# Gated delta rule in a decoder layer: block turns of v and of the output, and the decay exponents, made another way

## The reference, cut to what matters

```python
qkv = silu(causal_depthwise_conv(concat([q, k, v]), conv_w))
g = cumsum(g.reshape(B, H, N, C), axis=-1)          # g = log of the decay, C = 64 tokens
decay = exp(where(causal, g[..., :, None] - g[..., None, :], -inf))
a_mat = where(strict, einsum('bhncd,bhnsd->bhncs', k_beta, k) * decay, 0.0)
sol = triangular_solve(a_mat + eye(C), concat([v * beta, k_beta * exp(g)]), unit_diagonal=True)
qk = einsum('bhncd,bhnsd->bhncs', q, k) * decay
# scan over chunks with a state S per head; then
o = rms_norm(o, norm_w) * silu(z)                   # goes into o @ w_branch_a
```

## Time and profile before

| | |
|---|---|
| three timed executions | 1939.5, 1939.63, 1939.84 us |
| span of the profiled execution, first to last instruction | 1937.5 us |
| busy: PE, PEld | 1922.7 us (99%), 1581.1 us |
| busy: DVE, ACT, POOL | 1365.1 us (70%), 935.0 us (48%), 101.1 us |
| granted TensorE clock, mean | 0.998 |
| DMA | 353.19 MB, mean 182 GB/s |

### The profile page before, as it was taken

How to read it: one execution, slowest core, us unless ns; L and a number is a source line. 1 busy time by engine, 2 the same in 40 slices (tenths; PEclk the granted TensorE clock), 3 DMA queues, 4 the chain that set the end, 5 groups by cost and what they waited for, 6 DMA issues and landing times.

```text
span 1937.5 us, 33061 instructions
## 1 busy us (share of the span) xinstructions
PE 1922.7 (99%) x11140; PEld 1581.1 (82%) x11140; DVE 1365.1 (70%) x1961; ACT 935.0 (48%) x1331; POOL 101.1 (5%) x296
## 2 busy tenths in 40 slices
PE   9999999999999999999999999999999999999997
PEld 7888887888888888888888888888888888888886
DVE  7779889797857777776566766577675466665556
ACT  6555565554455545455544445644443444443442
POOL 0102020010101111111000000000000000000000
PEclk9999999999999999999999999999999999999999
DMA  7444444444554545455655676555555555656555
GB/s 267 154 142 158 149 152 142 154 153 142 186 179 159 188 161 191 159 189 174 190 192 194 216 239 200 181 194 191 191 194 195 194 193 188 196 195 194 194 189 174
DMA packets 98013, 353.19 MB, mean 182 GB/s; under 512 B 10832, under 2 KB 11120, under 8 KB 97776
## 3 DMA queue, kind: packets, MB, share of 16 engines
q1 hardware_dynamic: 97904, 351.65, 55.4%
HBM read 349.51 MB, written 2.10 MB: 181 GB/s over the span
## 4 chain that ended last, share of the span: by engine, by line
PE 95%; DVE 2%; ACT 1%; issue 1%; DMA 1%; SPq 0%; DVEq 0%; ACTq 0%
PE pg L399 88%; PE B L399 5%; DVE gates L1212 1%; DMA raw<-in_weights 1%; PE B L493 0%; ACT whi L800 0%; DVE wlo L1204 0%; PE B L657 0%; ACT hraw L1086 0%; PE B L527 0%; ACT gates L1074 0%; PE B L666 0%; PE B L622 0%; ACT vda L1086 0%; ACT act_a L800 0%
## 5 line engine op out<-in xcount | busy, mean ns | idle before, releaser
L1204 DVE TENSOR_TENSOR wlo<-raw,whi 128x1024 fp32r<-128x1024 f32 (+1 forms) x640 | 779.4, 1221 | 452.1 <-ACT whi L800 433.8
L800 ACT ACTIVATE whi<-raw 128x1024 fp32r<-128x1024 f32 (+1 forms) x640 | 674.4, 1058 | 684.6 <-PE pg L399 673.0
L399 PE MATMUL pg<-whi,act_x 128*128 128x512 f32 x2960 | 950.5, 394 | 1.5 <-ACT whi L800 1.2
L399 PEld LDWEIGHTS pg<-whi,act_x 128*128 128x128 f32 x2960 | 555.3, 188 | 124.3 <-issue 8.9
L399 PE MATMUL pg<-wlo,act_x 128*128 128x512 f32 x1480 | 574.7, 390 | 0.0
L399 PE MATMUL pg<-whi,act_a 128*128 128x512 f32 x1632 | 504.8, 389 | 0.5 <-DVE act_a L1204 0.5
L399 PEld LDWEIGHTS pg<-whi,act_a 128*128 128x128 f32 x1632 | 306.3, 188 | 64.8 <-DVE act_a L1204 1.3
L399 PEld LDWEIGHTS pg<-wlo,act_x 128*128 128x128 f32 x1480 | 278.3, 188 | 53.3
L399 PE MATMUL pg<-wlo,act_a 128*128 128x512 f32 x816 | 317.5, 389 | 0.0
L399 PEld LDWEIGHTS pg<-wlo,act_a 128*128 128x128 f32 x816 | 153.2, 188 | 31.7
L399 PE MATMUL pg<-whi,act_b 128*128 128x512 f32 x512 | 158.4, 389 | 0.0
(11 more groups left out here) (230 smaller groups left out, 1106.5 us busy)
## 6 DMA issues: line engine op xcount, KB each, us to landing
raw<-in_weights SPq DMA_DIRECT2D x646, 512.0 KB, 3.8
gates<-in_ln_in SPq DMA_DIRECT2D x4, 512.0 KB, 5.9
gates<-in_ln_in SPq DMA_DIRECT2D x1, 2048.0 KB, 8.4
out<-gates SPq DMA_DIRECT2D x8, 256.0 KB, 2.8
raw<-in_weights SPq DMA_DIRECT2D x4, 256.0 KB, 4.6
cT<-in_xT SPq DMA_DIRECT2D x2, 512.0 KB, 7.2
qT<-in_xrow SPq DMA_DIRECT2D x2, 512.0 KB, 7.4
kT<-in_xrow SPq DMA_DIRECT2D x2, 512.0 KB, 6.3
```

What stands on the lines that cost most here:

```text
L399: return nc.tensor.matmul(o, l, r, start=start, stop=stop)
L800: return nc.scalar.activation(o, i, ACT.Copy, scale=scale)
L1204: return V.tensor_tensor(o, a, b, op)
```

## The change

v: one VectorE transpose of 32x32 blocks over all 128 partitions (slot 20) writes `stage`. SP stores `stage` to `turn_v` in DRAM, waits until it is stored, and loads it back with the blocks in their new places, as four transfers of 32 partitions each. The rows are scaled from there in slots 26 and 30 (before: behind the last turn in slot 31, and in slot 0 of the next body). The output of head groups 0 to 2: two such transposes (slot 11 of the next body), the same way through `turn_o` to `oT`, split in slots 24 and 25 (before: 29 and 30). Decays: one small product in body 0 gives every running sum of g; ScalarE stores its transpose to DRAM, and one broadcast transfer per body, started by ScalarE, fills `decm` with it. ScalarE then does a Relu of `g - sum` for each of 8 tiles of 128x128 and one exponential over all of them: in bodies 1 to 3 two Relus in each of slots 4 to 7 and the exponential in slot 7, in body 0 all of it in slot 13. The masks `g_hi`, `g_lo`, the 4 products and the old exponential are gone.

```diff
-OT_TURN = {11: 3, 12: 4, 14: 2, 18: 1, 20: 3, 21: 3}
-OT_HI = 29
-V_TURN = {21: 1, 22: 3, 23: 3, 27: 3, 28: 2, 29: 2, 30: 1, 31: 1}
+O_BLOCKS, V_BLOCKS = 11, 20
+O_HI = 24
+V_SCALED = (26, 30)
...
-ROWS = range(2, 6)
+DECAY = range(4, 8)
...
+        stage = tmp("stage", [P, 4, 8, SB])
+        oT = tmp("oT", [P, 4, 8, SB])
...
+        centre, sums = (flat(QKT[:, :, :])[:, i * P:(i + 1) * P] for i in range(2))
+        vtok = flat(kT[:, :, :]).rearrange("p (a q x) -> p a q x", a=4, x=SB)
+        turn_v, turn_o = (nc.dram_tensor(n, (4, SB, 4, 8 * SB), F32).ap() for n in ("turn_v", "turn_o"))
+        sums_out = nc.dram_tensor("sums_out", (NB, 8 * P), F32).ap()
...
-            with sp.Fori(2, out_m) as m:
+
+            def blocks_out(scratch, kept):
+                sp.dma_start(scratch.rearrange("a x b c -> (a x) (b c)"), stage[:, :, :, :].rearrange("p b q x -> p (b q x)")
+                             ).then_inc(kept, 16)
+
+            def blocks_in(scratch, dst, full):
+                for b in range(4):
+                    sp.dma_start(dst[b * SB:(b + 1) * SB], scratch[:, :, b].rearrange("a x (q i) -> x a q i", i=SB)
+                                 ).then_inc(full, 16)
+
+            def v_out(j):
+                sp.wait_ge(N["dve_vS"], 1 + j + 1)
+                blocks_out(turn_v, v_kept)
+
+            def v_in(j):
+                sp.wait_ge(v_kept, 16 * (j + 1))
+                blocks_in(turn_v, vtok, v_full)
+
+            def o_out(j):
+                sp.wait_ge(N["dve_oS"], 1 + j)
+                blocks_out(turn_o, o_kept)
+
+            def o_in(j):
+                sp.wait_ge(o_kept, 16 * j)
+                blocks_in(turn_o, oT, o_full)
+
+            for m in range(2, 7):
+                later(m)
+            v_out(0)
+            later(7, range(0, 2))
+            v_in(0)
+            later(7, range(2, 4))
+            with sp.Fori(1, NB) as j:
+                for i in range(3):
+                    later(8 * j + i)
+                later(8 * j + 3, range(0, 3))
+                o_out(j)
+                later(8 * j + 3, range(3, 4))
+                later(8 * j + 4, range(0, 1))
+                o_in(j)
+                later(8 * j + 4, range(1, 4))
+                later(8 * j + 5)
+                later(8 * j + 6)
+                v_out(j)
+                later(8 * j + 7, range(0, 2))
+                v_in(j)
+                later(8 * j + 7, range(2, 4))
+            with sp.Fori(NB * BODY // RING, out_m) as m:
...
+                    mm(B[3][:, 64:96], centre, g_all[:, :]).then_inc(N["pe_sc0"], 1)
+                if s == 9:
+                    pe.wait_ge(N["act_gc"], 1)
+                    nc.tensor.transpose(B[3][0:SB, P:2 * P], pz[:, 1, :], ident).then_inc(N["pe_gT"], 1)
...
-                if s == 12:
-                    pe.wait_ge(N["rows"], 1 + j + 1)
-                    if isinstance(j, int):
-                        pe.wait_ge(N["act_glo"], 1)
+                if s == 13:
+                    pe.wait_ge(N["act_silu"], 1 + 3 * j + 1)
...
-                    for t in range(TOK):
-                        mm(B[1 + t][:, :], after_r[:, :], flat(g_hi[:, 4 * t:4 * t + 4, :]), True, False)
-                        last = mm(B[1 + t][:, :], after_r[:, :], flat(g_lo[:, 4 * t:4 * t + 4, :]), False, True)
-                    last.then_inc(N["pe_dt"], 1)
-                if s == 13:
-                    pe.wait_ge(N["act_silu"], 1 + 3 * j + 1)
-                    pe.wait_ge(N["act_decay"], 1 + j + 1)
...
+                    for t in range(TOK):
+                        by_t = B[3][:, 64 + HEADS * t:64 + HEADS * (t + 1)].rearrange("p (j h) -> p j h", h=HB)
+                        a0 = SC["gc"][0] + 4 * t
+                        copy(scal[:, :, a0:a0 + 4], by_t)
+                        last = copy(pz[:, 1, :].rearrange("p (j t h) -> p j t h", j=NB, t=TOK)[:, :, t, :], by_t)
+                    last.then_inc(N["act_gc"], 1)
+                if s == 10:
+                    act.wait_ge(N["pe_gT"], 1)
+                    copy(sums[0:SB, :], B[3][0:SB, P:2 * P]).then_inc(N["act_gT"], 1)
+                    act.wait_ge(N["act_gT"], 1)
+                    act.dma_start(sums_out.rearrange("j (i c) -> (j i) c", c=P), sums[0:SB, :]).then_inc(sums_kept, 16)
+                if s == 11:
+                    act.wait_ge(sums_kept, 16)
+                    sums_in(0)
+
+            def sums_in(j):
+
+                act.wait_ge(N["dve_qk"], 1 + 2 * j)
+                act.dma_start(flat(decm[:, :, :]), sums_out[bass.ds(j, 1)].rearrange("o c -> (o c)").partition_broadcast(P)
+                              ).then_inc(sums_full, 16)
...
+            def decays(j, part, parts):
+
+                if part == 0:
+                    act.wait_ge(sums_full, 16 * (j + 1))
+                    act.wait_ge(N["dve_g"], 1 + j + 1)
+                for i in range(8 // parts * part, 8 // parts * (part + 1)):
+                    last = nc.scalar.activation(decm[:, i, :], decm[:, i, :], ACT.Relu, bias=gcur[:, i:i + 1], scale=-1.0)
+                if part == parts - 1:
+                    last.then_inc(N["act_past"], 1)
+                    act.wait_ge(N["act_past"], 1 + j + 1)
+                    nc.scalar.activation(decm[:, :, :], decm[:, :, :], ACT.Exp, scale=-1.0).then_inc(N["act_decay"], 1)
+
             def dn_build(j, s):
-                if s in ROWS and not isinstance(j, int):
-                    per = 16 // len(ROWS)
-                    if s == ROWS[0]:
-                        act.wait_ge(N["dve_g"], 1 + j + 1)
-                        act.wait_ge(N["pe_dt"], 1 + j)
-                    for i in range(per * (s - ROWS[0]), per * (s - ROWS[0] + 1)):
-                        last = nc.scalar.activation((g_hi if i < 8 else g_lo)[:, i % 8, :], c("same"), ACT.Copy,
-                                                    scale=gcur[:, i:i + 1])
-                    if s == ROWS[-1]:
-                        last.then_inc(N["rows"], 1)
-                if s == 12:
-                    act.wait_ge(N["pe_dt"], 1 + j + 1)
-                    act.wait_ge(N["dve_qk"], 1 + 2 * j)
-                    for t in range(TOK):
-                        last = nc.scalar.activation(decm[:, 4 * t:4 * t + 4, :], B4[1 + t], ACT.Exp)
-                    last.then_inc(N["act_decay"], 1)
...
+                    if isinstance(j, int):
+                        decays(j, 0, 1)
...
-                if not alone and s == OT_HI:
-                    act.wait_ge(N["dve_od"], 1 + j + 1)
-                    copy(hi(act_a, HB * j, HB), qT[:, :, :]).then_inc(N["act_oT"], 2)
+                if not alone and s == O_HI:
+                    act.wait_ge(o_full, 64 * (j + 1))
+                    copy(by_block(hi(act_a, HB * j, HB)), by_source(oT)).then_inc(N["act_oT"], 2)
...
+                if s == 10:
+                    dve.wait_ge(N["act_gc"], 1)
+                    g_next(0)
...
-                if s in V_TURN:
-                    at = sum(n for k, n in V_TURN.items() if k < s)
-                    if at == 0:
-                        dve.wait_ge(N["act_silu"], 1 + 3 * j + 2)
-                    for i in range(at, at + V_TURN[s]):
-                        a, b = divmod(i, 4)
-                        ins = V.transpose(heads_of(kT)[b * SB:(b + 1) * SB, :, :, a, :],
-                                          tokens_of(cT[:, 1])[a * SB:(a + 1) * SB, :, :, b, :])
-                    if i == 15:
-                        ins.then_inc(N["dve_vT"], 1)
+                if s == V_BLOCKS:
+                    dve.wait_ge(N["act_silu"], 1 + 3 * j + 2)
+                    if not isinstance(j, int):
+                        dve.wait_ge(o_kept, 16 * j)
+                    V.transpose(stage[:, :, :, :].rearrange("p b q x -> p q b x"),
+                                cT[:, 1].rearrange("p h (q b x) -> p (h q) b x", q=TOK, x=SB)).then_inc(N["dve_vS"], 1)
+                if s in V_SCALED:
+                    if s == V_SCALED[0]:
                         dve.wait_ge(N["pool_rinv"], 1 + j + 1)
-                        dve.wait_ge(N["dve_vT"], 1 + j + 1)
-                        v_scaled(j, 0)
+                        dve.wait_ge(v_full, 64 * (j + 1))
+                    v_scaled(j, V_SCALED.index(s))
...
+                if not alone and s == O_BLOCKS:
+                    dve.wait_ge(N["dve_oh"], 1 + 2 * j + 2)
+                    dve.wait_ge(v_kept, 16 * (j + 1))
+                    for t in range(TOK):
+                        last = V.transpose(stage[:, :, :, :].rearrange("p b (h t) x -> p h t b x", t=TOK)[:, :, t],
+                                           od[:, t].rearrange("p h (b x) -> p h b x", x=SB))
+                    last.then_inc(N["dve_oS"], 1)
...
+                if not alone and s == O_HI + 1:
                     dve.wait_ge(N["act_oT"], 1 + 2 * j + 2)
-                    tt(lo(act_a, HB * j, HB), qT[:, :, :], hi(act_a, HB * j, HB), ALU.subtract).then_inc(N["dve_oT"], 2)
```

(46 more changed lines are left out.)

37 lines of the change are left out of this document (16 added, 21 removed).

## The result

The changed kernel takes 1972.05 us (median of 5, 1970.47 to 1974.4) against 1939.84 (5, 1939.5 to 1939.99): ratio 1.0168, 95% interval 1.0157 to 1.018. Slower was forecast, but at 1954 us with 1966 as the upper end; the loss is 32.2 us where 14.4 were forecast. The way was right, the size wrong.

The account below looks back on a forecast made before the run. TensorE, busy 1922.7 of 1937.5 us, was taken as the bound. To 1939.6 us it added 11.4 for bodies 1 to 3 and 2.6 for body 0, TensorE's savings included: 1953.6, stated as 1954 us; range 1942 to 1966.

Parts of the forecast that it names:

- What bounds, what TensorE saves: TensorE bounds; dropping four products per body saves 3.7 us, body 0's additions cost 0.2 to 0.3: net -3.5 us.
- VectorE's saving is worth nothing: Fewer block transposes remove about 39 us of VectorE work, worth nothing on TensorE.
- SP's hold: Bodies 1 to 3: the output store waits on SP's queue ahead of tiles 15 to 17; +3.8 us per body.
- the likeliest case: The forecast as worked out, both stalls present, 1954 us; chance 0.66.
- the landing: Tiles 15 and 16 in slot 11: 3.8 us from issue, plus 0.6 behind a store; bounds 3.0 to 5.3 for a load.
- `Pc`, 0.8 us in each body and 1.1 in body 0: After `Tc`, TensorE waits for VectorE's `Pc`: 0.8 us in each of bodies 1 to 3, 1.1 in body 0.
- At nothing: v's transfers, the broadcast of the sums and the output's split in slots 24 and 25 were covered, costing nothing.
- Slot 7: Bodies 1 to 3: ScalarE's Relus, 1.28 us table load and exponential delay its eviction, still 0.3 us ahead of TensorE's need.
- Slot 13 of body 0: Decays delay tile 17's split by 4.0 us; TensorE waits 2.2 for `Tc`, 1.1 for `Pc`; net +2.6 us.
- The second case: Rival: dearer transfers, stores taking 5 or 6 us to confirm, cost +6 to +8 per body: 1963 us; chance 0.17.
- The third: Rival: loads land in under 2 us, bodies 1 to 3 save 0.93 each, only body 0 pays: 1939.4 us; chance 0.08.
- the fourth: Rival: both stalls are covered and only TensorE's 3.5 us count: 1936.1 us; chance 0.09.

Follow-up runs that it names:

- body 0 mended: Changed kernel with SP's store and loads at their own slots, VectorE's moved work put back, and body 0's decays made earlier (slots 12 and 13): 1936.65 us.
- the old turns: v and the output turned by 16 block transposes each, as before the change: 1940.84 us with the changed decays, 1937.93 us with body 0's decays made earlier.
- the mended kernel: Changed kernel with both places mended: output store and loads at their own slots on SP's queue, VectorE's moved split and scalings put back: 1940.19 us.

## Why the prediction was right and wrong

Two steps failed most: every product was priced at full clock, and the work moved on VectorE was put at nothing. In the terms of the sum, measured against forecast: the waits in slot 14 are 15.7 us against 11.7, `Pc` 0 against 3.5, the wait for `Tc` 2.3 against 2.2, the waits in slot 28 5.9 against nothing, the lower clock 10.6 against nothing, and the saving of 3.5 is as forecast. Together 31.0 against 13.9.

- **What bounds, what TensorE saves.** Right. With body 0 mended 3.0 us come back with the transfers and 1.7 with the old turns; TensorE's busy time is 1919.9 us in the first of them, 2.8 less than before.
- **VectorE's saving is worth nothing.** Right to within about 1 us, by the runs with the old turns. The two wide turns take 1.30; 1.4 was taken.
- **SP's hold.** The mechanism and its place were right, and this was the likeliest case. The term "it waits 285.7 - 281.8 = 3.9 us" was too small: 5.7, 4.4 and 5.6 us. The step under it that failed is the landing, 4.4 and 4.7 us for tiles 15 and 16, with 5.3 as the bound for a load. Tile 15 took 4.2 to 4.8, but tile 16 lands 6.4 us after its issue in body 1 (169.07 to 175.5). I let oT's loads delay tile 17 alone; they run beside tile 16 too, and with those loads later it lands after 5.0.
- **`Pc`, 0.8 us in each body and 1.1 in body 0.** Wrong in bodies 1 to 3: no such wait appears. The longer wait in slot 14 and the slow products behind it hold TensorE back, and VectorE gets that time: in body 1 `Tc` ends at 187.96 and TensorE gets there at 191.36, where 0.3 us were forecast between the two. In body 0 the wait for `Pc` is there in the mended kernel (0.8); in the changed one it is not, behind a tile 18 that takes 1.6 us longer.
- **The clock.** This is the first thing the sum lacked. It priced every product at the durations of the earlier trace rows, read where TensorE had not stood, also those that stand directly behind a wait of 4 us, which the prediction itself put there. 10.6 us, a third of the loss.
- **"At nothing."** This is the second. The split of the output and the scaling of v were looked at only for whether their data would be there in time (it was). That they are 1.9 us more in front of `Tc`, the convolution of q and `Pm` was not priced: 5.9 us of waits, and 1.6 for the lower clock behind one of them. The trace of before would have shown it. In the rows of its body 1 above, `Pm` ends at 220.40 and the products start 0.15 us later; in the changed kernel, where they wait for `Pm`, they start 0.15 us behind it too (234.06 and 234.21). So they already started as early as `Pm` let them.
- **Slot 7.** Right: TensorE does not wait in slot 8. ScalarE's eviction ends at 154.58 in body 1 and the transposes behind it start at 154.99, 0.4 us later. So the table load costs its 1.28 us and no drain beside it; the Trainium skill's 2.66 ("ScalarE: Activation LUTs", What ACT_TABLE_LOAD costs), 1.38 more, would have shown as a wait there. In the rows of body 0 above, too, the exponential follows its load by 0.02 us.
- **Slot 13 of body 0.** Right for the wait (2.3, forecast 2.2); the tile behind it ran at the lower clock.
- **The rivals.** The second case ("the transfers cost more") named 21 us for bodies 1 to 3 and gave them to the store's confirmation; stores land in 2.9 us, so it fails on its own reason. That its 1963 is nearer to the result is luck. The third (only body 0 pays) and the fourth (faster) fail on the wait in slot 14. The range ended at 1966 because it knew no cost beyond the second case's.

## What to carry to other kernels

On an engine that is never idle, price a wait twice: the time until its releaser comes, and the work behind it at the lower clock, as it ran behind all three waits of slot 14. When work is moved to earlier slots, ask not only whether its inputs are ready but what stands behind it on that engine, and how much room the consumer of that had in the trace. On a queue that starts transfers in order, put each statement that waits behind all those whose condition comes earlier: two statements three slots too early cost 25 us here, and what they carried was worth 1.3 at the most in the pairs with the old turns.

## What the runs showed that I had not expected

Eighteen extra products of 128x512 ahead of each of three waits made the kernel 7.9 us faster. The lower clock did not follow every wait: in the kernel with both places mended the same 2.3 us of idle time in body 0 is followed by a tile at full speed (2.95 us, clock 1.00 from 60 to 80 us), in the changed kernel by one of 4.54 us. No run here shows what decides between the two.
